# Decoder layer with pooling, dilated attention and 32 experts: router ahead of the second norm, gather tile made on ScalarE, seeds and weight loads moved

## The chip, the cores and the metric

The kernel runs on one core of one Trainium2 chip. The metric is the device time of one execution in microseconds (us). TensorE has an HBM-fed stream of weights beside it, which SyncE issues as DMAs.

## The reference, cut to what matters

One layer, 256 tokens, 1024 channels, everything in f32:

```python
u = layer_norm(x) * (1.0 + scale1) + shift1
...                                            # projection, pooling, attention, gates -> merged
mix = merged @ w_o
x = layer_norm(DN_ALPHA * x + (1.0 + gate1) * mix, ln1_g, ln1_b)
u2 = layer_norm(x) * (1.0 + scale2) + shift2
logits = u2 @ w_router + b_router              # 32 experts, top 4 of them per token, softmax over the 4
# each expert e, for its tokens: h = g * sigmoid(1.702 g) * (up + 1), g = min(u2 @ w_gate + b, 7), ...
ffn = weighted sum over the 4 experts of h @ w_down + b_down
x = layer_norm(DN_ALPHA * x + (1.0 + gate2) * ffn, ln2_g, ln2_b)
```

The three weight matrices of all 32 experts are 4 MB each and are all read: 384 MB.

## The kernel before

The 256 tokens are two tiles of 128 (t = 0, 1). The five engines run hand-written instruction lists side by side and meet at semaphores; `step` on VectorE lets every instruction wait for the one before it.

**Front (0 to 199 us).** Norm, projection, attention and pooling give `gates` (merged, feature-major). Then, in the order of TensorE's list:
- L1449: mix = merged @ w_o, tile by tile, in halves of 512 columns into banks 2 to 5. A logical f32 matmul shows as two passes in the profile.
- L1462: eight transposes of u2 of tile t into banks 6 and 7 (u2 lives in ln_tok, as `xn`). L1470: the rows of gate2, after tile 0. L1477: the router's eight matmuls; L1479: one more that adds the shift and bias row (`shift_sum`) to the logits.
- L1486: the seed of tile t, which puts DN_ALPHA * x into two of banks 0 to 3, onto which the experts' results are added later. L1456: `keep_busy`, dummy matmuls; four (eight passes) after tile 0.
- L1494 to L1497: ranks of the tokens within each expert from the chosen mask and a triangular matrix. L1502: `gather`, which multiplies u2 with a one-hot matrix, so that M_BANK holds the up to 64 tokens of one expert, feature-major. L1558: transposes of the weights per token.
- L1519: `stream`, a unit of the expert's weights (a quarter of 1024 x 1024 is a tile; a unit is four tiles of 512 KB, half a matrix) against those tokens. Six units make one expert: gate 0, 1, up 2, 3, down 4, 5. Between them lie the next expert's gather and the transposes of h (L1540), whose columns are read with a stride of four values.

**VectorE around the change.** For each tile and half: mix times gate1 (L1003), plus DN_ALPHA * x (L1005), statistics (L1008). Then `scaled_norm` (L843: aggregate L845, L846, reciprocal L849, L852, statistics of the result L855), which needs the rows of ln1, and `plain_norm` (L857: aggregate L858, reciprocal L860, and u2 in two halves, L863). Only after both tiles follow the top four of each tile from its logits: max, index, cast, comparison, reduction, cast (L1018 to L1027), then the rank (L1029), `pick_expert` (L1035), and the weights (L1055 to L1060, reduction of 256 values at L1060). ScalarE takes the roots (`norm_std`, L707), copies the transposed tile (L711), makes gate2's rows and the scaled identity (L727, L728), the exponentials of the top four (L717), and turns the gathered tile into the experts' input with scale2 and shift2 (`select_tile`, L737).

**Loads.** SyncE issues the weights in one fixed list and waits for each place to become free. The ring has eight slots of one unit; beside it, units 8 and 9 go to two extra places for the first two turns: `ln_rows` and `x_tok` (extra 0), `late_rows` and `spare_tile` (extra 1). So ten units can be ahead. Slots 4 and 5 (units 4 and 5 of expert 0) become free with the last branch matmul, slots 0 and 1 (units 6, 7) with the mix. In extra 0, `ln_rows` is free when u2 is made and `x_tok` after both seeds (L524, L526). The units 10 and 11 are loaded tile by tile as unit 0 and 1 of expert 0 are used up (L540), every later one when the unit before it in its place is used (L544):

```python
sp.wait_ge(pe_unit_used, AT_PLACE[place - SLOTS] + 1)
sp.dma_start(expert_view(place), source(u)).then_inc(slot_landed[RING[place % SLOTS]], 16)
```

The rows of ln1 are issued by ScalarE once `merged` is complete (L699).

## Time and profile before

| | us |
|---|---|
| median of 3 executions | 1167.73 (1167.57 to 1167.88) |
| the profiled execution | 1166.89 |
| its span, first to last instruction | 1165.0 |
| TensorE busy, passes of weights and matmuls | 1126.5 (97%) |
| VectorE busy | 345.1 (30%) |
| ScalarE busy | 127.3 (11%) |
| DMA over the span | 462.01 MB, mean 397 GB/s |

Times in the profile are counted from the first instruction. An engine's busy time is the union of its instructions; a releaser behind an arrow is the work that ended the wait. PE is TensorE, PEld its weight loads, DVE VectorE, ACT ScalarE, POOL GpSimd, SPq SyncE's list of DMA issues. The granted clock of TensorE has a mean of 0.997 of full speed.

### The profile page before, as it was taken

Reading aid. Unit: us, or ns where it says so; the run is one execution under the profiler, and the core shown is the slowest. Engines: PE = TensorE matmul, PEld = TensorE weight load, DVE = VectorE, ACT = ScalarE, POOL = GpSimd, SP = SyncE. Lnnn points to the kernel's source line nnn. Section 1 sums busy time; section 2 is a strip of 40 time slices with the busy share of each in tenths; the row PEclk is TensorE's granted clock in tenths of the full one; section 3 lists DMA queues with packets and bytes.
Section 4 is the critical chain, followed back from the end, with each engine's and each line's share of the span. In section 5 each row is a group of like instructions: output and inputs, shape, how many; then the busy total and the mean of one; then the engine's idle time right before and its main releaser. Section 6 shows DMA issues by size and latency. Waiting matters only on the chain.

```text
span 1165.0 us, 13496 instructions
## 1 busy us (share of the span) xinstructions
PE 1126.5 (97%) x5821; PEld 553.7 (48%) x5821; DVE 345.1 (30%) x628; ACT 127.3 (11%) x227; POOL 20.1 (2%) x28
## 2 busy tenths in 40 slices
PE   6999999999999999999999999999999999999996
PEld 4868887454444444444444444444444444444442
DVE  4297963642222211211221112221211121112113
ACT  2113221130001000000000000001000100000001
POOL 0000400000000000000000000000000000000000
PEclk9999999999999999999999999999999999999998
DMA  9999685789999999999999999999999999999994
GB/s 346 387 352 353 242 331 230 283 307 394 426 426 427 425 427 425 429 426 429 434 430 430 431 431 432 432 432 432 432 430 431 432 431 432 432 425 427 426 420 196
DMA packets 53732, 462.01 MB, mean 397 GB/s; under 512 B 5294, under 2 KB 7214, under 8 KB 34746
## 3 DMA queue, kind: packets, MB, share of 16 engines
q1 hardware_dynamic: 50032, 457.19, 94.3%
q10 hardware_dynamic: 3658, 4.20, 1.1%
q8 instruction: 34, 0.56, 0.2%
q14 instruction: 8, 0.07, 0.0%
HBM read 460.33 MB, written 1.05 MB: 396 GB/s over the span
## 4 chain that ended last, share of the span: by engine, by line
PE 75%; DMA 21%; DVE 3%; SPq 1%; issue 0%; ACT 0%; DVEq 0%; ACTq 0%
PE bank L1519 43%; DMA ring<-w_up 19%; PE bank L1502 8%; PE bank L1350 6%; PE bank L1546 4%; PE bank L1287 4%; PE bank L1651 2%; PE bank L1435 2%; PE bank L1344 2%; DMA pool_region<-ln_b 1%; DMA ring<-w_in 1%; PE bank L1540 1%; PE bank L1527 1%; SPq L475 1%; PE bank L1508 1%; PE bank L1375 0%
## 5 line engine op out<-in xcount | busy, mean ns | idle before, releaser
L1519 PE MATMUL bank<-ring,feat_region 128*64 128x512 f32 x2848 | 625.2, 595 | 14.3 <-DMA ring<-w_up 14.3
L1519 PEld LDWEIGHTS bank<-ring,feat_region 128*64 128x64 f32 x2848 | 199.5, 137 | 415.7 <-issue 394.9
L1502 PEld LDWEIGHTS bank<-row_region,ln_tok 128*128 128x128 f32 x1024 | 116.8, 192 | 20.3 <-issue 19.7
L1502 PE MATMUL bank<-row_region,ln_tok 128*128 128x64 f32 x1024 | 121.1, 277 | 0.2 <-DVE row_region L1035 0.2
L1100 DVE TENSOR_TENSOR gate_region<-bank,row_region 128x512 f32<-128x512 f32 x31 | 21.4, 691 | 249.4 <-PE bank L1519 249.4
L1078 DVE TENSOR_SCALAR gate_region<-bank 128x512 f32<-128x512 f32 x31 | 21.4, 691 | 200.9 <-PE bank L1527 200.9
L1090 DVE TENSOR_SCALAR acc_region<-bank 128x512 f32<-128x512 f32 x31 | 21.4, 692 | 170.6 <-PE bank L1527 170.6
L1350 PE MATMUL bank<-feat_region,ring 128*128 128x256 f32 x320 | 70.6, 381 | 0.0
L1546 PE MATMUL bank<-gate_region 64*128 64x512 f32 x264 | 65.9, 616 | 0.8 <-DVE gate_region L1123 0.8
L1350 PEld LDWEIGHTS bank<-feat_region,ring 128*128 128x128 f32 x320 | 60.4, 190 | 10.9 <-issue 3.1
L753 ACT ACTIVATE gate_region<-bank 128x256 f32<-128x256 f32 x31 | 11.9, 383 | 470.1 <-PE bank L1508 470.1
L758 ACT ACTIVATE feat_region<-bank 128x512 f32<-128x512 f32 x31 | 18.5, 597 | 331.6 <-PE bank L1540 331.6
L1287 PE MATMUL bank<-feat_region,ring 128*128 128x256 f32 x192 | 42.4, 381 | 1.1 <-DMA ring<-w_in 1.1
L1095 DVE TENSOR_TENSOR feat_region<-bank,small 128x512 f32<-128x512 f32 x31 | 21.4, 691 | 69.0 <-PE bank L1502 69.0
L1287 PEld LDWEIGHTS bank<-feat_region,ring 128*128 128x128 f32 x192 | 36.2, 190 | 6.9 <-DMA ring<-w_in 1.3
L1546 PEld LDWEIGHTS bank<-gate_region 64*128 64x128 f32 x264 | 22.6, 186 | 22.0 <-issue 16.5
L1449 PE MATMUL bank<-ring,gate_region 128*128 128x512 f32 x64 | 27.6, 593 | 0.0
L879 DVE SCALAR_TENSOR_TENSOR row_region<-ring,small,row_region 128x512 f32<-128x512 f32 x32 | 27.1, 848 | 1.1
L1527 PE MATMUL bank<-bias_parts,attn_region 96*64 96x512 bf16 x128 | 25.5, 391 | 0.0
L879 DVE SCALAR_TENSOR_TENSOR acc_region<-ring,small,acc_region 128x512 f32<-128x512 f32 x32 | 24.1, 752 | 1.1
L1088 DVE TENSOR_TENSOR acc_region<-acc_region,gate_region 128x512 f32<-128x512 f32 x31 | 21.3, 686 | 5.8 <-ACT acc_region L756 5.8
L1097 DVE TENSOR_TENSOR feat_region<-feat_region,small 128x512 f32<-128x512 f32 x31 | 21.5, 692 | 1.1
(240 smaller groups left out, 611.9 us busy)
## 6 DMA issues: line engine op xcount, KB each, us to landing
ring<-w_gate SPq DMA_DIRECT2D x16, 4096.0 KB, 27.6
ring<-w_up SPq DMA_DIRECT2D x16, 4096.0 KB, 30.6
ring<-w_down SPq DMA_DIRECT2D x16, 4096.0 KB, 31.7
ring<-w_gate SPq DMA_DIRECT2D x28, 2048.0 KB, 15.5
ring<-w_up SPq DMA_DIRECT2D x26, 2048.0 KB, 15.2
ring<-w_down SPq DMA_DIRECT2D x26, 2048.0 KB, 17.9
ring<-w_ada SPq DMA_DIRECT2D x8, 2048.0 KB, 15.9
ring<-w_in SPq DMA_DIRECT2D x6, 2048.0 KB, 13.9
```

The costliest lines, as they stand in the source:

```text
L879: ins = nc.vector.scalar_tensor_tensor(out=acc, in0=w[:, k, :], scalar=c_silu[:, k:k + 1], in1=acc, op0=ALU.mult, op1=ALU.add)
L1097: nc.vector.tensor_tensor(x_sel, x_sel, shift2.unsqueeze(2).to_broadcast([P, KT, CAP]), ALU.add) \
L1287: last = nc.tensor.matmul(dst[:, q * S:(q + 1) * S], w[:, k, f * P:(f + 1) * P], u_t[:, k, :], start=(q, k) == (0, 0), stop=(q, k) == (1, ...
L1344: last = nc.tensor.matmul(dst[:, cols], u_t[:, k, t * P:(t + 1) * P], w[:, k, :], start=k == 0, stop=k == KT - 1)
L1350: last = nc.tensor.matmul(dst[:, q * S:(q + 1) * S], w[:, k, f * P:(f + 1) * P], u_t[:, k, :], start=k == 0, stop=k == KT - 1)
L1435: last = nc.tensor.matmul(bank[b + n % 2][:, q * S:(q + 1) * S], w[:, k, f * P:(f + 1) * P], src[:, k, :], start=k == 0, stop=k == kk - 1)
L1449: last = nc.tensor.matmul(bank[2 + 2 * t + hf][:, :], gates[:, k, t * P:(t + 1) * P], unit_view(u)[:, k % 4, hf * HALF:(hf + 1) * HALF], s ...
L1502: last = nc.tensor.matmul(M_BANK[:, k * CAP:(k + 1) * CAP], u2[:, t, k * P:(k + 1) * P], pick_tok[:, b, t, :], start=t == 0, stop=t == NT - 1)
L1519: last = nc.tensor.matmul(dst[hf * CAP:(hf + 1) * CAP, :], lhs(k0 + k), cols(tiles[k], hf), start=first and k == 0, stop=last_one and k == 3)
L1527: last = nc.tensor.matmul(dst[hf * CAP:(hf + 1) * CAP, :], pick_bias[:, b, :], half_cols(bias_parts[:, which, :], hf), start=False, stop=stop)
L1546: last = nc.tensor.matmul(bank[2 * t + hf][:, :], scatter_t[rows, b, t, :], values[rows, :], start=False, stop=stop)
L1651: last = nc.tensor.matmul(dst[hf * CAP:(hf + 1) * CAP, :], lhs(4 * (k % 2) + kt), cols(tiles[kt], hf), start=first and kt == 0, stop=last_ ...
```

## The change

1. `scaled_norm` writes its last step in two parts that hold four of the eight feature tiles each (strided columns), signals each (`z_ready`), and only then takes the statistics. TensorE transposes x_tok itself (columns 32 bytes apart), not u2, into `u2_t` in gate_region, and multiplies with the router.
2. The logits are put right afterwards: VectorE adds minus the mean times the column sums of the scaled router, multiplies with the reciprocal root and adds the shift row. Both rows are summed over the partitions by one matmul after the first part of the mix; the matmul of the shift row per tile goes.
3. `second_norm` computes mean and reciprocal root only. ScalarE makes u2, in two activations of 1024 values per tile, after its copies for the router. The root of the second norm of tile 1 comes behind those copies.
4. Mix of tile 1: parts of 512, 256 and 256 columns (banks 4, 5, 0), statistics of tile 1 in quarters.
5. The top four are compared straight with the index (no cast) for both tiles; the picks themselves (bf16) go to the rank matmuls (twelve, not three); the reduction over k is one of 256 values.
6. TensorE's list: the seed of tile 0 waits for all parts of the mix to be read; three dummy matmuls instead of four; the first expert's gather is split into two halves (banks 7 and 6), the second half, the transposes of the weights and the seed of tile 1 lie inside the gate stream of expert 0.
7. Loads: extra 0 is feat_region and ln_rows in place of ln_rows and x_tok. Its first half is issued when the last gate job is done, late_rows ahead of slot 4, the rows of ln1 by SyncE between slots 4 and 5, and extra 0's second half when the moments of the second norm of tile 1 are there. x_sel, h and h_t move to gate_region.

```diff
-        extra_tiles = [[ln_rows[:, 0, :], ln_rows[:, 1, :], x_tok[:, 0, :], x_tok[:, 1, :]],
+        feat_rows = feat_region[:, :].rearrange("p (k n) -> p k n", k=2)
+        extra_tiles = [[feat_rows[:, 0, :], feat_rows[:, 1, :], ln_rows[:, 0, :], ln_rows[:, 1, :]],
...
+        mix_parts = [[(0, HALF, bank[2]), (HALF, D, bank[3])],
+                     [(0, HALF, bank[4]), (HALF, HALF + S, bank[5]), (HALF + S, D, bank[0])]]
...
-            for m in range(SLOTS - 2):
+            for m in range(4):
                 fill_slot(m)
+            sp.wait_ge(job_done, JOB_POOL)
+            sp.dma_start(feat_rows, source(SLOTS)[:, 0:2, :]).then_inc(extra_landed[0], 16)
             sp.wait_ge(job_done, JOB_POOL + 2)
             sp.wait_ge(router_scaled, 1)
             sp.dma_start(late_rows, source(SLOTS + 1)[:, 0:3, :]).then_inc(extra_landed[1], 16)
+            fill_slot(4)
             sp.wait_ge(merged, KT // 2)
+            for r, w in enumerate((ln1_g, ln1_b)):
+                sp.dma_start(ln_rows[:, r, :], w.to_broadcast([P, D])).then_inc(ld_ln1, 16)
+            fill_slot(5)
             sp.dma_start(spare_tile, source(SLOTS + 1)[:, 3, :]).then_inc(extra_landed[1], 16)
             for m in range(SLOTS - 2, SLOTS):
                 fill_slot(m)
-            sp.wait_ge(u2_ready, 2 * NT)
-            sp.dma_start(ln_rows, source(SLOTS)[:, 0:2, :]).then_inc(extra_landed[0], 16)
-            sp.wait_ge(seeded, 2 * NT)
-            sp.dma_start(x_tok[:, :, :], source(SLOTS)[:, 2:4, :]).then_inc(extra_landed[0], 16)
+            sp.wait_ge(moments_ready, 2 + 2 * NT)
+            sp.dma_start(ln_rows, source(SLOTS)[:, 2:4, :]).then_inc(extra_landed[0], 16)
...
+            def u2_tile(t):
+                act.wait_ge(norm2_ready, t + 1)
+                tile = u2[:, t, :].rearrange("p (k a) -> p k a", k=KT)
+                nc.scalar.activation(tile, x_tok[:, t, :].rearrange("p (a k) -> p k a", k=KT), ACT.Identity,
+                                     bias=minus_mean[:, t:t + 1]).then_inc(act_chain, 1)
+                act.wait_ge(act_chain, t + 1)
+                nc.scalar.activation(u2[:, t, :], u2[:, t, :], ACT.Copy, scale=rstd[:, t:t + 1]).then_inc(u2_ready, 1)
...
             for b in range(2):
                 u2_t_half(1, b)
+            norm_std(1, 1)
+            u2_tile(1)
+            nc.scalar.activation(small[:, 102:103], eps, ACT.Exp)
...
+                step(nc.vector.scalar_tensor_tensor(out=row, in0=scale_row, scalar=minus_mean[:, t:t + 1],
+                                                    in1=bank[4 + t][:, 0:NE], op0=ALU.mult, op1=ALU.add), moe_chain)
+                step(nc.vector.scalar_tensor_tensor(out=row, in0=row, scalar=rstd[:, t:t + 1], in1=shift_row,
+                                                    op0=ALU.mult, op1=ALU.add), moe_chain)
...
                     if k % 4 == 0:
-                        pe.wait_ge(u2_ready, 2 * t + k // 4 + 1)
+                        pe.wait_ge(z_ready, 2 * t + k // 4 + 1)
                     last = nc.tensor.transpose(bank[6 + k // 4][:, (k % 4) * P:(k % 4 + 1) * P],
-                                               u2[:, t, k * P:(k + 1) * P], ident)
+                                               x_tok[:, t, :].rearrange("p (a k) -> p k a", k=KT)[:, k, :], ident)
...
                 if t == 0:
-                    keep_busy(4)
+                    pe.wait_ge(scaled_ready, 1)
+                    pe.wait_ge(mix_read, MIX_PARTS)
+                    seed(0)
+                    keep_busy(3)
...
             pe.wait_ge(picked, 1)
-            gather(0).then_inc(gather_done, 1)
-            pe.wait_ge(weight_ready, 1)
+            pe.wait_ge(u2_ready, NT)
+            first_gather(0)
+
+            def weights_and_seed():
+                pe.wait_ge(weight_ready, 1)
...
+                pe.wait_ge(gate2_ready, 1)
+                seed(1)
...
+                               between=(lambda: first_gather(1), weights_and_seed)[k] if first and j == 0
+                               else None) \
```

## Rows read from the trace of the kernel before

**Rows 1.** windows view, two long stretches (window, then busy us of each engine, granted clock, DMA share, GB/s)
```profile
273.00:728.00 455.00, 455.00 (x2382) 194.18 (x2378) 93.99 (x177) 35.73 (x56) 0.00 (x0) 1.00 1.00 428
728.00:1100.00 372.00, 358.94 (x1880) 153.80 (x1878) 75.69 (x143) 25.79 (x43) 0.00 (x0) 1.00 1.00 431
```

**Rows 2.** DMA view of 180 to 300 us, 40 slices of 3 us
```profile
GB/s 426 426 186 0 5 0 87 355 415 414 401 401 352 65 0 55 311 431 437 336 218 309 8 318 314 363 427 352 404 431 262 306 431 426 431 426 437 418 423 442
```

**Rows 3.** windows view, slices of 2 us
```profile
270.00:272.00 2.00, 2.00 (x12) 0.58 (x9) 0.00 (x0) 0.00 (x0) 0.00 (x0) 1.00 0.67 287
272.00:274.00 2.00, 2.00 (x12) 0.72 (x10) 0.00 (x0) 0.00 (x0) 0.00 (x0) 1.00 0.68 139
```

**Rows 4.** timeline of the DMA issues on SyncE (start us, us, line, what)
```profile
248.20 6.34 SPq L540 DMA_DIRECT2D ring<-w_down  x8
258.39 3.76 SPq L544 DMA_DIRECT2D ring<-w_gate  x2
271.79 3.76 SPq L544 DMA_DIRECT2D ring<-w_up  x2
```

**Rows 5.** timeline of TensorE from 226 to 255 us (xcount of passes)
```profile
226.68 1.04 PE L1462 MATMUL bank<-const,ln_tok 128*128 128x128 f32 x8
...
228.65 1.97 PE L1477 MATMUL bank<-router_w,feat_region 128*128 128x32 f32 x16
230.46 0.39 PE L1479 MATMUL bank<-router_w,const 128*128 128x32 f32 x2
231.10 1.99 PE L1486 MATMUL bank<-x_tok,acc_region 128*128 128x512 f32 x4 [0.25 <-ACT acc_region L728]
232.92 3.21 PE L1456 MATMUL bank<-const 128*128 128x454 f32 x8
236.25 1.46 PE L1462 MATMUL bank<-const,ln_tok 128*128 128x128 f32 x8
237.69 1.94 PE L1477 MATMUL bank<-router_w,feat_region 128*128 128x32 f32 x16
...
242.72 3.79 PE L1502 MATMUL bank<-row_region,ln_tok 128*128 128x64 f32 x32 [0.19 <-DVE row_region L1035]
246.43 0.63 PE L1558 MATMUL bank<-const,attn_region 128*32 128x128 f32 x8
247.09 7.09 PE L1519 MATMUL bank<-ring,feat_region 128*64 128x512 f32 x32
...
254.33 0.44 PE L1508 MATMUL bank<-const,row_region 128*128 128x128 f32 x2
```

**Rows 6.** timeline of VectorE, steps around tile 1 and the top four
```profile
218.29 0.21 DVE L845 BATCH_NORM_AGGREGATE small<-small 128x2 f32<-128x12 f32 x1 [2.93 <-DMA pool_region<-ln_b]
...
227.65 0.69 DVE L1003 TENSOR_TENSOR ln_tok<-bank,row_region 128x512 f32<-128x512 f32 x1
...
229.83 0.21 DVE L845 BATCH_NORM_AGGREGATE small<-small 128x2 f32<-128x12 f32 x1
...
239.96 0.20 DVE L1018 MAX8 attn_region<-bank 128x8 f32<-128x32 f32 x1 [1.08 <-PE bank L1479]
...
242.11 0.23 DVE L1029 SCALAR_TENSOR_TENSOR attn_region<-bank,attn_region 128x64 f32<-128x64 f32 x1 [0.30 <-PE bank L1497]
242.37 0.29 DVE L1035 TENSOR_TENSOR row_region<-const,attn_region 128x128 f32<-128x128 f32 x1
...
243.43 0.60 DVE L1060 TENSOR_REDUCE attn_region<-attn_region 128x64 f32<-128x256 f32 x1
```

**Rows 7.** lines 1462 and 1540, weight loads (ns min/median/max), and the first transposes of h
```profile
L1462 PEld LDWEIGHTS bank<-const,ln_tok x16: 138/141/146, 226.2 to 237.3; 128*128 128x128 f32 x16
...
L1540 PEld LDWEIGHTS bank<-const,feat_region x20: 212/216/233, 265.5 to 377.3; 128*128 128x128 f32 x20
...
265.56 0.68 PE L1540 MATMUL bank<-const,feat_region 128*128 128x128 f32 x4
```

**Rows 8.** timeline of ScalarE, a copy of 512 values
```profile
236.94 0.60 ACT L711 ACTIVATE feat_region<-bank 128x512 f32<-128x512 f32 x1 [0.28 <-PE bank L1462]
```

More of the change, by code:

```diff
@@ L1007, in _ @@
                                                         op0=ALU.mult, op1=ALU.add))
-                    step(nc.vector.bn_stats(stats[:, t, hf, :], x_tok[:, t, cols]))
+                    if t == 0:
+                        step(nc.vector.bn_stats(stats[:, t, n, :], x_tok[:, t, cols]))
+                    else:
+                        for q in range(c0 // S, c1 // S):
+                            step(nc.vector.bn_stats(last_stats[:, q, :], x_tok[:, t, q * S:(q + 1) * S]))
                 dve.wait_ge(ld_ln1, 32)
-                scaled_norm(t, 2 + 2 * t + 1)
@@ new lines, in _ @@
+                step(nc.vector.max(top_v[:, t, :], row), moe_chain)
+                step(nc.vector.max_index(top_i[:, t, :], top_v[:, t, :], row), moe_chain)
+            dve.wait_ge(acc_read, 8)
+            for t in range(NT):
+                step(nc.vector.tensor_tensor(picks[:, t], experts,
+                                             top_i[:, t, 0:TOP_K].unsqueeze(2).to_broadcast([P, TOP_K, NE]),
+                                             ALU.is_equal), picks_ready)
+            step(nc.vector.tensor_reduce(chosen_f, picks.rearrange("p t k e -> p t e k"), AX.X, ALU.add), moe_chain)
@@ L1028, in _ @@
+            step(nc.vector.tensor_scalar(top_n.unsqueeze(2), top_v[:, :, 0:1], -1.0, None, ALU.mult), top_ready)
             dve.wait_ge(rank_done, 1)
@@ L1190, in _ @@
                 dve.wait_ge(final_std, t + 1)
-                final(nc.vector.reciprocal(rstd[:, t:t + 1], std[:, t:t + 1]))
+                step(nc.vector.reciprocal(rstd[:, t:t + 1], std[:, t:t + 1]))
                 for hf in range(2):
@@ L1456, in keep_busy, with seed @@
                     nc.tensor.matmul(bank[b][:, 0:columns], ident, const[:, 0:columns], start=True, stop=True)
+            pe.wait_ge(row_sums_ready, 2)
+            def seed(t):
+                for n in (2 * t, 2 * t + 1):
+                    nc.tensor.matmul(bank[n][:, :], scaled_ident, x_tok[:, n // 2, (n % 2) * HALF:(n % 2 + 1) * HALF],
+                                     start=True, stop=False)
             for t in range(NT):
@@ new lines, in _ @@
+            keep_busy(1, 3, S)
+            for t in range(NT):
+                pe.wait_ge(picks_ready, t + 1)
+                if t == 0:
+                    for k in range(TOP_K):
+                        nc.tensor.matmul(Y_BANK[:, 0:NE], tri_bf, picks[:, 0, k, :],
+                                         start=k == 0, stop=k == TOP_K - 1)
+                for k in range(TOP_K):
+                    last = nc.tensor.matmul(Y_BANK[:, NE:2 * NE], tri_bf if t else one_bf[:, 0:1].to_broadcast([P, P]),
+                                            picks[:, t, k, :], start=(t, k) == (0, 0), stop=(t, k) == (1, TOP_K - 1))
@@ L1499, in gather, with gather_tile @@
+            last.then_inc(rank_done, 1)
+            def gather_tile(dst, b, k):
+                for t in range(NT):
+                    last = nc.tensor.matmul(dst, u2[:, t, k * P:(k + 1) * P], pick_tok[:, b, t, :],
+                                            start=t == 0, stop=t == NT - 1)
+                return last
             def gather(b):
                 for k in range(KT):
-                    for t in range(NT):
-                        last = nc.tensor.matmul(M_BANK[:, k * CAP:(k + 1) * CAP], u2[:, t, k * P:(k + 1) * P],
-                                                pick_tok[:, b, t, :], start=t == 0, stop=t == NT - 1)
@@ L1504, in gather, with first_gather @@
-                return last
+                    last = gather_tile(M_BANK[:, k * CAP:(k + 1) * CAP], b, k)
+                return last
+            def first_gather(half):
+                for k in range(4 * half, 4 * half + 4):
+                    last = gather_tile(FIRST_GATHER[half][:, (k % 4) * CAP:(k % 4 + 1) * CAP], 0, k)
+                return last.then_inc(first_gathered, 1)
             def transpose_scatter():
@@ L1513, in out_cols, with stream @@
                 return tile[:, hf * HALF:(hf + 1) * HALF]
-            def stream(dst, lhs, tiles, k0, first, last_one, cols=half_cols, tile_done=None):
+            def stream(dst, lhs, tiles, k0, first, last_one, cols=half_cols, tile_done=None, between=None):
                 for k in range(4):
+                    if k == 2 and between is not None:
+                        between()
                     for hf in range(2):
```

205 lines of the change are left out of this document (92 added, 113 removed).

## The prediction

> **What bounds the kernel now.** I read the long stretches first. From 273 to 728 us TensorE has no gap, and the DMA moves 428 GB/s. From 728 to 1100 us TensorE is busy 358.94 of 372 us, and the DMA moves 431 GB/s [rows 1]. TensorE walks through one expert in about 27.9 us, and the 12.58 MB of an expert's weights take 29.2 us at 431 GB/s. So TensorE, which begins with ten units of two megabytes in place, uses that lead up until 728 us and waits for weights from there. The DMA is the limit in both stretches. The end is therefore the moment at which the DMA stands idle for the last time, plus all that is still to be loaded. A microsecond won on TensorE after that moment is worth nothing.
>
> So the second view is the DMA over 180 to 300 us, in slices of 3 us [rows 2]. It is empty from 189 to 201 us, from 219 to 227 us, and around 247 us. The reader might add these holes up. They don't count by themselves, though: ten units of weights (two megabytes each, six to an expert) are all that fits ahead, and each later unit waits for TensorE to free a place. The last hole is the short one at 270 to 274 us, where the share is 0.67 and 0.68 [rows 3]. What ends it is the issue at 271.79 us [rows 4], which waited for TensorE to finish unit 4 of expert 0 (the first half of its down projection). Both units of the up projection were freed by 261.8 us, their refills (4.9 us each) ran out by 271, and then the queue was empty. From 274 us it is never empty again: TensorE frees 12.58 MB per 27.9 us, the DMA needs 29.2. Remaining bytes agree: the first 14 of 192 units aside, 374 MB at 429 GB/s are 872 us, from 273 to 1145.
>
> **So one number decides:** when TensorE comes to unit 4 of expert 0. From the end of expert 0's gate stream (the transposes of the scatter at 254.33 us [rows 5]) to there, nothing is changed by the edit. I follow TensorE to that point in both kernels.
>
> **What lies around it.** In the kernel before, VectorE waits 2.93 us for the rows of ln1 [rows 6], is 0.5 us late for the last part of the mix (227.65 us, where TensorE is already at the next transposes at 226.68), and then holds TensorE until 236.25 us with both norms. TensorE fills this time with router matmuls of tile 0, the seed of tile 0 and eight dummy passes, which end as the second norm ends: transposes of tile 1 at 236.25 us [rows 5].
>
> **The change, part by part, on TensorE.**
> 1. Mix. One matmul of 64 columns for the row sums (two passes; like the passes of the gather, 3.71 us for 32, 0.12 us each) adds 0.25 us. Sixteen passes of 512 columns become 32 of 256: between nothing and 0.3 us more (a weight load of 190 ns must hide behind a pass of 216), I take 0.15. Transposes of tile 0 start 0.40 us later: 227.08.
> 2. Transposes now read x_tok with 32 bytes between elements; u2 was contiguous. Rows 7 show both kinds: the contiguous weight load takes 141 ns, the one of h, 16 bytes apart, 216 ns. Eight contiguous passes last 1.04 us in all [rows 5], 0.13 each; four of h 0.68 [rows 7], 0.17 each. With only four the end of the last weighs more, so I take 0.035 of the 0.04 (bounds: nothing, and the whole 75 ns). Eight here: +0.28. Transposes and gate2 rows took 1.97 us (226.68 to 228.65), now 2.25: router matmuls of tile 0 start at 229.33.
> 3. They took 1.81 us (228.65 to 230.46): 231.14. The matmuls of the shift row fall away, and the wait for the scaled identity too: it followed the aggregate of tile 1 (229.83, [rows 6]) by 1.27 us. With ln1 early VectorE is free when the mix ends; a last part of 256 columns costs about 0.45 us per step instead of 0.73, so that aggregate comes at 228.75 and the identity at 230.0. Seed of tile 0: 231.10 to 232.92 before, 1.82 us, now until 232.96. Six dummy passes instead of eight, 0.38 each: 2.29, until 235.25. VectorE has the tile for the router (both halves written) at about 232.1: the aggregate, 1.28 us, the reciprocal, and twice 0.78. So the bound changes hands here. **TensorE itself is late by three microseconds**, and of the four that VectorE is earlier (236.2 to 232.1) it sees 1.00 (236.25 to 235.25).
> 4. Tile 1: transposes to first router matmul 1.44 us, plus four strided transposes, 0.14: 236.83. Router matmuls to VectorE's first step 2.27 us (237.69 to 239.96), less two passes: 2.04, so 238.87, where it was 239.96. ScalarE takes the root only behind its two copies (0.60 each [rows 8], to 237.2); then VectorE needs 0.4 and 1.0 us for tile 0, done at about 238.9. Nothing lost, with no room left.
> 5. VectorE, from there to the gather. Before: 2.76 us (239.96 to 242.72). Now: two steps on 32 values (0.23 each), max and index (0.54), two comparisons (0.29 and step costs, 0.66), the reduction, now of 256 values and ahead of the ranks (0.60, [rows 6]), the negation (0.18), rank (0.26), pick to gather (0.35): 3.05. Copy, cast and one reduction are gone. The ranks' twelve small matmuls run beside the reduction. Gather at 241.95, 0.8 us earlier. ScalarE's u2 for tile 1: from 237.8, two activations of 1024 elements; twice the 0.60 us of 512 is the upper bound, so ready by 240.3. Hidden by 1.6 us.
> 6. First half of the gather 1.86 us, then 0.66 us to the first weight tile (246.43 to 247.09): the gate stream starts at 244.47, **2.6 us earlier** than before.
> 7. Inside that stream now lie the other half of the gather (1.86), the weights' transposes (0.66), and the seed of tile 1 (1.82), which before ran at 239.7 to 241.7 us beside VectorE's top four and cost nothing. Its cover is gone. 7.24 + 4.34 us: the stream is through at 256.05 where it was 254.33. **TensorE is 1.7 us later.**
>
> **The DMA's own changes** cost and give nothing. Half of extra unit 0 into feat_region at 176 us and the three late tiles at 179 us fill some six microseconds of the first hole, the same bytes are then missing behind 214 us, and the second hole grows. The rows of ln1, behind fill 4 only, are there by about 209 us, needed at 215.4. The second half of extra unit 0 leaves at about 234 us. Tile releases of unit 0 come earlier (248.20 before), so their refills are through sooner, and the queue stands empty for longer before unit 4. What is late next is this release, at 271.8 + 1.7 = 273.5 us.
>
> **Sum.** The profiled execution took 1166.89 us (span 1165.0), 0.84 below the median of 1167.73. 1166.89 + 1.7 = 1168.6, against the median 1169.4.
>
> A rule weighed against it: the Trainium skill, SBUF — State Buffer, Door 1, says that memory lines have 16 bytes and every access that crosses to a new line pays. By it 32 bytes apart costs what 16 bytes cost, as I took it; by the contiguous price alone the sum would be 0.4 less. VectorE's step that reads x_tok at this stride takes 0.75 us, like those that read it contiguously, so on that engine the trace shows no such cost.
>
> **The rivals.**
> A. Early release counts: expert 0 starts 2.6 us earlier and the holes filled early pay. Then 1167.7 - 2.6 = 1165.1, faster. For it: three large holes [rows 2]. Against: the hole at 270 to 274 lies behind all of them. It needs my TensorE sum to be wrong by over 3 us. Chance 0.15, with all else that ends below.
> B. It cancels: TensorE's passes are shorter at steps 1, 2 and 7 (a pass of 454 columns takes 0.38 us, so four of 512 at 0.43 make a seed of 1.73; contiguous price for transposes, no cost for halves), some 0.9 less: 1168.5 to 1167.8. No change. Chance 0.2.
> C. Slower, by the strided weight loads: if 32 bytes cost twice the surcharge of 16 (150 ns, not 75), and all of it shows, 0.075 us more each than I took: 0.6 more at tile 0, 0.3 at tile 1, since TensorE is the late engine there. 1170.3. It decides from about 0.06 us more each on. For it: 216 against 141 ns; against: no row shows a load at 32 bytes, and as many values are read. Chance 0.15, with small steps mis-sized upwards.
> D. ScalarE's u2 comes late: only if an activation with this stride takes over 2.0 us, 1.6 us of room is used up; at 2.6 us each the gather waits 1.2 more: 1170.6. Chance 0.05.
> E. The clock: it is granted in full in every stretch around [rows 1, 3], and gaps of up to 1.0 us don't lower it. Now TensorE waits for some 1.7 of 3 us before the gather. If it fell to 1.2 GHz over the first half gather and two tiles, they would take 3.6 us more: 1173.0. Chance 0.05. The Trainium skill, TensorE: Matmul & The Clock Gate, Part 1, says that idle time halves the clock and work restores it; by it this risk exists, and no row here shows matmuls at the lower level.
>
> **How the numbers follow.** About 0.2% (2.3 us) is what a measurement of this kernel can tell from no change: 1165.4 and 1170.1. The forecast, TensorE 1.0 to 2.5 us later, has 0.40 and its own range 1168.7 to 1170.2, nearly all within the bound. Faster: A, 0.15. Same: forecast 0.37 and B 0.20. Slower: C, D, E and the forecast's edge, 0.28. The range takes in A's price and leaves out E: 1165.1 to 1171.4.
>
> **What would show it.** Right: TensorE's transposes of tile 1 follow the dummy passes without a wait, while VectorE has written the tile about 3 us earlier; their weight loads near 216 ns; gate stream from about 244.5 us but ending near 256; the DMA's last hole before the issue for unit 4, now near 273.5; from there everything moved by the same amount. Wrong: a gate stream ending before 254, no hole near 272, or a hole later than this one.

## The result and the profile after

The changed kernel takes 1172.81 us (median of 5 executions, 1172.00 to 1173.95), the kernel before 1167.73 us (5 executions beside it on the same chip, 1166.23 to 1168.25). The ratio is 1.0047, with a 95% interval of 1.0036 to 1.0058: **slower, by 5.1 us**, where 1169.4 was forecast. The profiled execution took 1172.81 us, with a span of 1171.0; of before, 1166.89 and 1165.0. The mean granted clock is 0.993, where it was 0.997. The span is 6.0 us longer, and that difference is to be explained. It is more than the 5.1 us of the medians, since the profiled execution of before was 0.84 us under its median and that of the changed kernel was not.

The first view is again the DMA's, the same 40 slices of 3 us as in [rows 2], and SyncE's issues, as in [rows 4]:

```profile
GB/s 426 431 418 438 280 0 55 339 392 389 410 378 4 0 0 0 279 431 431 412 199 0 3 217 165 380 320 317 180 421 431 371 60 311 415 431 437 437 437 410
```

```profile
248.08 12.50 SPq L554 DMA_DIRECT2D ring<-w_down  x8
264.43 3.76 SPq L558 DMA_DIRECT2D ring<-w_gate  x2
277.82 3.76 SPq L558 DMA_DIRECT2D ring<-w_up  x2
```

The reader is to see the last hole: slice 33 (276 to 279 us) with 60 GB/s, where it was slice 31 with 262. Unit 4 of expert 0 is let go at 277.82 us. It was 271.79, so 6.03 us later, and the span grew by 6.0. From the release to the end there are 893.2 us in both kernels (1165.0 - 271.79, 1171.0 - 277.82). So the number that the prediction followed decides, and what is left is why TensorE had finished unit 4 only at 277.82 us and not at 273.5.

TensorE's timeline from the mix to the end of the first gate stream, as in [rows 5]:

```profile
227.33 1.04 PE L1493 MATMUL bank<-const,x_tok 128*128 128x128 f32 x8
...
229.31 1.97 PE L1508 MATMUL bank<-router_w,gate_region 128*128 128x32 f32 x16
231.12 1.96 PE L1486 MATMUL bank<-x_tok,acc_region 128*128 128x512 f32 x4
232.92 2.45 PE L1481 MATMUL bank<-const 128*128 128x454 f32 x6
235.20 1.05 PE L1493 MATMUL bank<-const,x_tok 128*128 128x128 f32 x8
236.59 1.94 PE L1508 MATMUL bank<-router_w,gate_region 128*128 128x32 f32 x16 [0.33 <-ACT gate_region L721]
238.36 0.68 PE L1481 MATMUL bank<-const 128*128 128x256 f32 x2
240.08 0.27 PE L1522 MATMUL bank<-acc_region,attn_region 128*128 128x32 bf16 x4 [1.04 <-DVE acc_region L1053]
...
240.52 1.02 PE L1481 MATMUL bank<-const 128*128 128x256 f32 x2
241.81 3.67 PE L1530 MATMUL bank<-row_region,ln_tok 128*128 128x64 f32 x16 [0.28 <-DVE row_region L1065]
246.07 3.68 PE L1559 MATMUL bank<-ring,gate_region 128*64 128x512 f32 x8 [0.59 <-ACT gate_region L761]
249.68 2.60 PE L1530 MATMUL bank<-row_region,ln_tok 128*128 128x64 f32 x16
252.21 3.65 PE L1559 MATMUL bank<-ring,gate_region 128*64 128x512 f32 x16
255.79 0.63 PE L1601 MATMUL bank<-const,attn_region 128*32 128x128 f32 x8
256.36 1.98 PE L1486 MATMUL bank<-x_tok,acc_region 128*128 128x512 f32 x4
...
260.37 0.44 PE L1546 MATMUL bank<-const,row_region 128*128 128x128 f32 x2
```

Up to the gather every start lies within 0.25 us of the step that forecast it: 227.33 for 227.08, 229.31 for 229.33, 231.12 for 231.14, 232.92 for 232.96, 235.20 for 235.25, 236.59 for 236.83, 241.81 for 241.95. Then the same instruction takes different times: sixteen passes of the gather 3.67 us and then 2.60; eight passes of the stream 3.68 us, sixteen 3.65. The two dummy passes of 256 columns take 0.68 us at 238.36 and 1.02 at 240.52. The windows say why (the granted clock is the third number from the end):

```profile
236.00:238.00 2.00, 1.67 (x16) 1.50 (x14) 0.69 (x4) 1.70 (x4) 0.00 (x0) 1.00 1.05 451
238.00:240.00 2.00, 1.04 (x7) 0.64 (x6) 1.66 (x9) 1.97 (x2) 0.31 (x1) 1.00 0.90 381
240.00:242.00 2.00, 1.65 (x15) 0.87 (x16) 1.59 (x6) 1.98 (x2) 0.00 (x0) 0.68 0.68 287
242.00:244.00 2.00, 2.00 (x11) 2.00 (x11) 1.06 (x4) 0.80 (x6) 0.00 (x0) 0.50 0.03 12
...
248.00:250.00 2.00, 2.00 (x8) 0.39 (x4) 0.00 (x0) 0.00 (x0) 0.00 (x0) 0.50 0.46 96
250.00:252.00 2.00, 2.00 (x15) 2.00 (x15) 0.00 (x0) 0.00 (x0) 0.00 (x0) 0.76 0.82 229
```

**The clock is at its lower level, 1.2 GHz, from about 240.7 to about 251 us.** Ahead of it TensorE is busy 1.04 of 2 us: it waits 1.04 us for the comparisons of tile 1 on VectorE, where the seed of tile 1 stood in the kernel before. This is rival E. Two lines of ScalarE and one of VectorE complete the view:

```profile
237.41 2.15 ACT L734 ACTIVATE ln_tok<-x_tok,small 128x1024 f32<-128x1024 f32 x1 [0.30 <-DVE small L886]
239.58 1.15 ACT L737 ACTIVATE ln_tok<-ln_tok,small 128x1024 f32<-128x1024 f32 x1
```

```profile
216.00 0.21 DVE L869 BATCH_NORM_AGGREGATE small<-small 128x2 f32<-128x12 f32 x1
```

ScalarE's strided activation takes 2.15 us and the contiguous one 1.15. u2 is nevertheless ready at 240.7, 1.1 us ahead of the gather. The wait for ln1 (2.93 us in [rows 6]) is gone, as the change means it to be.

### The profile page after: what moved, and what is told of

Same layout as the page of the kernel before. It is cut to its first block, busy times and chain, and to the rows that moved or that the text cites. A ratio compares the mean times of both kernels' runs of the same rounds, so it can differ in the third digit from the quotient of the medians.

```text
span 1171.0 us, 13544 instructions
## 1 busy us (share of the span) xinstructions
PE 1131.2 (97%) x5844; PEld 558.7 (48%) x5844; DVE 343.6 (29%) x629; ACT 134.0 (11%) x233; POOL 20.7 (2%) x28
## 3 DMA queue, kind: packets, MB, share of 16 engines
HBM read 460.33 MB, written 1.05 MB: 394 GB/s over the span
## 4 chain that ended last, share of the span: by engine, by line
PE 78%; DMA 19%; DVE 2%; ACT 0%; issue 0%; DVEq 0%; ACTq 0%
PE bank L1559 43%; DMA ring<-w_up 19%; PE bank L1530 8%; PE bank L1371 6%; PE bank L1586 4%; PE bank L1308 4%; PE bank L1470 2%; PE bank L1699 2%; PE bank L1456 2%; PE bank L1365 2%; PE bank L1580 1%; PE bank L1567 1%; PE bank L1289 1%; PE bank L1546 1%; DMA small<-c 0%; PE bank L1396 0%
## 5 line engine op out<-in xcount | busy, mean ns | idle before, releaser
L1559 PE MATMUL bank<-ring,gate_region 128*64 128x512 f32 x2848 | 627.4, 596 | 14.8 <-DMA ring<-w_up 14.2
L1559 PEld LDWEIGHTS bank<-ring,gate_region 128*64 128x64 f32 x2848 | 199.2, 137 | 416.9 <-issue 396.2
L1530 PE MATMUL bank<-row_region,ln_tok 128*128 128x64 f32 x1024 | 123.6, 280 | 0.3 <-DVE row_region L1065 0.3
L782 ACT ACTIVATE gate_region<-bank 128x512 f32<-128x512 f32 x31 | 18.5, 597 | 331.5 <-PE bank L1580 331.5
L1125 DVE TENSOR_TENSOR gate_region<-bank,small 128x512 f32<-128x512 f32 x31 | 21.4, 691 | 68.9 <-PE bank L1530 68.9
L1470 PE MATMUL bank<-ring,gate_region 128*128 128x512 f32 (+1 forms) x80 | 27.9, 508 | 0.0
L1122 DVE SCALAR_TENSOR_TENSOR gate_region<-acc_region 128x512 f32<-128x512 f32 x31 | 21.5, 692 | 1.1
```

The lines of the kernel that those rows point to most:

```text
L1122: nc.vector.scalar_tensor_tensor(out=h, in0=up_c, scalar=1.0, in1=sig, op0=ALU.add, op1=ALU.mult).then_inc(h_ready, 1)
L1470: last = nc.tensor.matmul(dst[:, 0:c1 - c0], gates[:, k, t * P:(t + 1) * P], unit_view(u)[:, k % 4, c0:c1], start=k == 0, stop=k == KT - 1)
L1530: last = nc.tensor.matmul(dst, u2[:, t, k * P:(k + 1) * P], pick_tok[:, b, t, :], start=t == 0, stop=t == NT - 1)
L1559: last = nc.tensor.matmul(dst[hf * CAP:(hf + 1) * CAP, :], lhs(k0 + k), cols(tiles[k], hf), start=first and k == 0, stop=last_one and k == 3)
```

## The experiments

Three questions: is it the pause ahead of the ranks that lowers the clock; what do the other parts (seed, halves, dummies, loads) cost or give; and does only the release of unit 4 count. Medians and ratios are against runs of the kernel before on the same chip.

### The pause filled

```diff
-            keep_busy(1, 3, S)
+            keep_busy(2, 3)
             for t in range(NT):
...
-            keep_busy(1, 4, S)
+            keep_busy(1, 4)
             pe.wait_ge(picked, 1)
```

> The changed kernel, with TensorE's wait between the router's last matmuls and the gather filled by more dummy passes (six passes of 454 columns in place of four of 256). Theory (the clock): the granted clock stays at 1.00 from 236 to 256 us, the first half of the gather takes 1.9 us instead of 3.7, the release of unit 4 comes near 273.5 us instead of 277.8, and the profiled span falls from 1171.0 to 1166.7 +- 0.6, 1168.5 in time. Rival (the clock falls for another cause, such as the small router and rank matmuls themselves): it falls to 0.50 again near 241 us and the span stays at 1171 or above.

Measured: span 1166.8 us, clock 0.998, median 1169.16 (1168.21 to 1171.08), ratio 1.0015 (1.0006 to 1.0024). TensorE and SyncE:

```profile
238.04 1.77 PE L1481 MATMUL bank<-const 128*128 128x454 f32 x4
...
241.50 2.00 PE L1530 MATMUL bank<-row_region,ln_tok 128*128 128x64 f32 x16 [0.29 <-DVE row_region L1065]
...
256.03 0.44 PE L1546 MATMUL bank<-const,row_region 128*128 128x128 f32 x2
```

```profile
273.49 0.33 SPq L558 DMA_DIRECT2D ring<-w_up  x1
```

Only dummy work was added, and 4.2 us of the span went (by the two ratios to the kernel before, 3.7). The half gather takes 2.00 us for 3.67, the gate stream ends at 256.03 where the prediction had 256.05, and unit 4 is let go at 273.49 where it had 273.5. Two small errors cancel in that match: the gather begins 0.45 us before the 241.95 of the prediction, and from the start of the stream to its end are 11.95 us, not 11.58. The miss of the changed kernel is the clock all the same: 277.82 - 273.49 = 4.33 us, of which 0.31 is an earlier front (all that lies ahead of the gather) in this execution (gather at 241.50) and 4.0 the lower level. Five of the ten executions lie at 1168.2 to 1168.7 us with a mean clock of 0.998, three at 1169.6 to 1169.8 with 0.997, and two near 1171 with 0.996, so the filling does not seem to hold the clock every time.

### The seed of tile 1 back in its old place

```diff
-            keep_busy(1, 3, S)
+            pe.wait_ge(gate2_ready, 1)
+            seed(1)
             for t in range(NT):
...
-                pe.wait_ge(gate2_ready, 1)
-                seed(1)
```

> The changed kernel, with the seed of tile 1 moved out of expert 0's gate stream to where it was before, between the router's last matmuls and the ranks. Theory (clock plus 1.8 us of uncovered work): the clock is held by real work in the gap, the gate stream of expert 0 ends near 254.1 us, unit 4 is released near 271.6, span 1164.8 +- 0.6, the kernel ends level with the one before. Rival (the clock needs more than this): 0.50 again, and the span only falls by the 1.8 us of the seed, to 1169.2. Rival (the seed's place is free because its passes were hidden): as with the dummies alone, 1166.7.

Measured: span 1164.7, release at 271.62 us; 1.87 us before the filled variant's. From the gather to the release are 30.08 us here and 31.99 in the filled variant, so the seed inside the stream costs 1.91 us. The median is 1168.96, ratio 1.0006 (0.9997 to 1.0015), and hides two groups: five executions at 1166.6 to 1167.2 us, all with a mean clock of 0.997, and five at 1169.0 to 1169.9 us with 0.995 or 0.996 (an eleventh at 1170.3, with 0.997). The profiled one is of the first group, so the trace doesn't show where the others lose the clock. The seed covers the pause ahead of the ranks; TensorE then still waits 0.62 us ahead of the gather and 0.59 behind its first half.

### The six dummy passes behind the first seed left out

```diff
                     seed(0)
-                    keep_busy(3)
```

This is the variant above without these three matmuls.

> As the one with the seed of tile 1 moved back, and without the six dummy passes behind the seed of tile 0, for which TensorE kept VectorE waiting. Theory (TensorE was the late engine there, by 2.9 us): transposes of tile 1 start near 232.9 us in place of 235.2, the gather near 239.6, unit 4 is released 2.2 us earlier than in that kernel, span 1162.6 +- 0.8, faster than the kernel before by 2.3 us. Rival (those passes held the clock): the clock falls to 0.50 somewhere between 233 and 245 us and takes back 3 to 4 us: span 1166 or more.

Measured: median 1165.40 (1164.34 to 1166.06), ratio 0.9978 (0.9969 to 0.9987), span 1163.8 with the front 0.64 us later in the profiled execution (transposes of tile 0 at 227.68), mean clock 0.997 or 0.998 in all eleven.

```profile
233.27 1.04 PE L1493 MATMUL bank<-const,x_tok 128*128 128x128 f32 x8
```

The transposes of tile 1 still have no wait, 2.3 us earlier against those of tile 0. The span is above the 1162.6 +- 0.8 that was expected: the late front is 0.64 us of that, and from the release (269.96) to the end are 893.8 us, 0.6 more than in the kernel before. What those 0.6 us are is not settled. **The dummies ran while VectorE's tile was ready**: it was written at 232.3 us in the changed kernel and TensorE took it up at 235.20. That the clock never falls here is measured; why it holds without these passes and falls in half of the executions with them is not settled.

### The loads issued in the old order

```diff
-            sp.wait_ge(job_done, JOB_POOL)
-            sp.dma_start(feat_rows, source(SLOTS)[:, 0:2, :]).then_inc(extra_landed[0], 16)
...
             fill_slot(5)
+            sp.wait_ge(router_scaled, 1)
+            sp.wait_ge(job_done, JOB_POOL + 2)
+            sp.dma_start(late_rows, source(SLOTS + 1)[:, 0:3, :]).then_inc(extra_landed[1], 16)
...
             sp.wait_ge(moments_ready, 2 + 2 * NT)
+            sp.dma_start(feat_rows, source(SLOTS)[:, 0:2, :]).then_inc(extra_landed[0], 16)
```

On top of the variant with the seed back (the rows of ln1 stay early).

> As the one with the seed of tile 1 moved back, but the early half of extra unit 0 and the three late tiles are issued where the kernel before had them (behind the moments of tile 1, and behind slot 5). Theory (only the release of unit 4 counts): the DMA's hole at 189 to 201 us is whole again, the one at 214 to 227 us shrinks, and the span is that of the kernel with the seed moved back, within 0.5 us. Rival (bytes moved into an early hole are won): 2.5 to 6 us slower than that kernel.

Measured: span 1164.9, release 271.67 (271.62 with the early loads), the same two groups (1166.4 to 1167.2 and 1169.0 to 1169.7 us), median 1168.09, ratio 1.0007 (0.9997 to 1.0016) against 1.0006 with the early loads. Filling the first hole early is worth nothing that these runs can tell.

### The kernel before with only the seed of tile 1 moved

```diff
                 if t == 0:
+                    seed(0)
                     keep_busy(4)
...
             last.then_inc(weight_t_done, 1)
+            pe.wait_ge(gate2_ready, 1)
+            seed(1)
```

> The kernel before, with one edit of the change alone: the seed of tile 1 is taken from between the router's last matmuls and the ranks and put behind the weights' transposes, ahead of expert 0. Theory (the uncovered seed and the wait it leaves, which lowers the clock): the granted clock falls to 0.50 near 241 us for about 10 us, unit 4 is released 1.8 + 4 us later, near 277.5, span 1170.8. Rival (the seed counts, the clock falls only with the changed kernel's smaller matmuls and longer wait): clock 1.00, span 1166.8.

Measured: median 1174.23 (1173.36 to 1174.46), ratio 1.0060 (1.0045 to 1.0075), span 1172.2, release 279.06, mean clock 0.991.

```profile
241.86 0.18 PE L1495 MATMUL bank<-attn_region 128*128 128x32 bf16 x1 [1.91 <-DVE attn_region L1026]
...
242.94 6.97 PE L1503 MATMUL bank<-row_region,ln_tok 128*128 128x64 f32 x32
249.84 1.07 PE L1559 MATMUL bank<-const,attn_region 128*32 128x128 f32 x8
250.84 3.59 PE L1484 MATMUL bank<-x_tok,acc_region 128*128 128x512 f32 x4
```

```profile
240.00:242.00 2.00, 0.14 (x4) 0.17 (x4) 1.64 (x8) 0.06 (x1) 0.00 (x0) 0.61 0.79 320
242.00:244.00 2.00, 2.00 (x11) 1.60 (x8) 1.65 (x6) 0.33 (x2) 0.00 (x0) 0.50 0.02 8
```

The old kernel's gather, 3.79 us in [rows 5], takes 6.97, its transposes 1.07 for 0.63, the seed 3.59 for 1.99. One move, with nothing else of the change, lowers the clock and costs more than the whole change does. It costs 1.4 us more than was expected, since the whole gather, the transposes and the seed all ran at the lower level: 3.2, 0.3 and 1.7 us more than at the full clock.

### Dummies early, later, and later still

Three dummy matmuls (six passes, 2.3 us) ahead of the next gather, in the kernel before: in expert 0, in expert 2, and in expert 8.

```diff
                     pe.wait_ge(picked, i * BODY + (j + 2))
+                    if first and j == 0:
+                        keep_busy(3, 7)
                     gather(1 - b)
```

(`j == 2` for expert 2; `at == 2 and j == 0` for expert 8.)

> The kernel before, with three dummy matmuls (six passes of 454 columns, 2.3 us) ahead of the gather inside expert 0, before its unit 4. Theory (the end is the release of unit 4 plus a constant): release near 274.1 us, span 1165.0 + 2.3 = 1167.3. Rival (TensorE's lead of several experts hides it): span 1165.0.

> The kernel before, with the same three dummy matmuls (2.3 us) in the same place of expert 2. Theory (behind the DMA's last hole TensorE's time is free): release of unit 4 of expert 0 unchanged at 271.8 us, span 1165.0 +- 0.4. Rival (every microsecond of TensorE up to 728 us counts): 1167.3.

> The kernel before with the same three dummy multiplications (2.3 us) in expert 8, behind both narrow places (release of unit 4 near 272 us, and the transfers near 440 us that the dummies in expert 2 opened). Theory: the transfers have a lead of several us there and are never idle, so the span is the release of unit 4 plus 893.2 us within 0.4 (1165 us if the front part runs as in the profiled execution of before). Rival (TensorE's own time after the front counts): 1167.3 or more by the same sum.

Measured: in expert 0 median 1169.37, ratio 1.0019 (1.0009 to 1.0028), release 274.99; in expert 2 median 1168.85, ratio 1.0012 (1.0002 to 1.0021), release 272.70; in expert 8 median 1167.52, ratio 0.9997 (0.9987 to 1.0006), release 271.80 and span 1164.9 = 271.80 + 893.1. In the profiled executions of the first two the front was 0.9 us late (the first issue behind it at 249.11, before 248.20), so expert 0's dummies moved the release by 274.99 - 272.70 = 2.29 us, what they last. Spans: 1168.2 and 1166.9. So early dummies cost their full time and the latest nothing, as the theory has it, but **those in expert 2 cost some of it**, which it did not foresee: 1166.9 - 272.70 = 894.2, not 893.2, so 1.0 of 2.3 us in the profiled execution (1.6 us by the medians). The windows of that kernel at 441 us:

```profile
441.00:442.00 1.00, 1.00 (x6) 0.29 (x4) 0.00 (x0) 0.00 (x0) 0.00 (x0) 1.00 0.43 180
442.00:443.00 1.00, 1.00 (x8) 0.40 (x6) 0.00 (x0) 0.00 (x0) 0.00 (x0) 1.00 0.27 115
```

```profile
442.24 3.76 SPq L544 DMA_DIRECT2D ring<-w_gate  x2
```

The two extra places are used for the first turns alone. Where they fall away, one issue comes 21 us behind the one before it; in the last kernel of the three, at 439.06, it still comes in time. That is a second narrow place, with a lead of about one microsecond (1.3 by this run: 2.3 us were lost and 1.0 showed). The release near 272 us ends the last hole only as long as TensorE loses little between the two.

### Needed work in place of the filler

The variant without the six dummy passes, and half of the first seed behind the ranks in place of the dummy there, and VectorE's negation moved behind the first pick.

```diff
-                    seed(0)
+                    seed(0, 0)
...
-            keep_busy(1, 4, S)
+            seed(0, 1)
             pe.wait_ge(picked, 1)
...
-            step(nc.vector.tensor_scalar(top_n.unsqueeze(2), top_v[:, :, 0:1], -1.0, None, ALU.mult), top_ready)
...
             pick_expert(0, 0).then_inc(picked, 1)
+            step(nc.vector.tensor_scalar(top_n.unsqueeze(2), top_v[:, :, 0:1], -1.0, None, ALU.mult), top_ready)
```

> As the one without the dummy passes (seed of tile 1 in its old place), with the second half of the seed of tile 0 behind the ranks in place of the dummy there, and the negation for the exponentials behind the first pick. Theory: transposes of tile 1 start when VectorE has the tile, 0.5 us earlier, the gather another 0.2 us, unit 4 is released 0.7 us earlier than in that kernel (measured from the first transposes of tile 0), span 1163.0 or below, 0.3 to 0.4% faster than the kernel before. Rival (the clock has no more room without the passes ahead of the transposes): it falls to 0.50 and the span is 1166 or more.

Measured: median 1164.73 (1163.53 to 1165.16), ratio 0.9979 (0.9970 to 0.9988), span 1161.7, clock 0.997 in all eleven executions.

```profile
238.13 2.00 PE L1530 MATMUL bank<-row_region,ln_tok 128*128 128x64 f32 x16
240.72 1.94 PE L1559 MATMUL bank<-ring,gate_region 128*64 128x512 f32 x8 [0.59 <-ACT gate_region L761]
```

```profile
268.21 3.76 SPq L558 DMA_DIRECT2D ring<-w_up  x2
```

Both seeds are now ahead of the gather, no filler is left there, and the gather begins 4.6 us before the old one's 242.72. From the first transposes of tile 0 (226.72 here, 227.68 in the variant without the dummies) to the release are 0.8 us less, as expected. The medians don't show it: the ratio is 0.9979, and 0.9978 for that variant on another chip, and the 0.3 to 0.4% that were expected are 0.2.

### The gather undivided

```diff
             first_gather(0)
+            first_gather(1)
...
-                               between=(lambda: first_gather(1), weights_and_seed)[k] if first and j == 0
+                               between=(None, weights_and_seed)[k] if first and j == 0
```

> d1_best with the first gather undivided again (all eight passes ahead of the stream, the weights and the last seed still behind unit 0). Theory (only the release of unit 4 counts): the eight passes are the same ones, so the first tile of unit 0 is let go about 2 us later, unit 4 at the same time within 0.5 us of d1_best's 268.21, and the span is 1161.7 within 0.5. Rival (the halves are worth something): the ring's transfers behind the first tile wait 2 us longer, and the span is 1163.5 or more.

Measured: median 1163.94 (1162.75 to 1163.97, 5 executions), ratio 0.9962 (0.9949 to 0.9975), span 1161.0, a little below the 1161.7 +- 0.5 that was expected: the lowest ratio of the study, 0.38% below before, though the intervals of the last two variants overlap.

```profile
238.43 3.79 PE L1530 MATMUL bank<-row_region,ln_tok 128*128 128x64 f32 x32
242.14 5.37 PE L1559 MATMUL bank<-ring,gate_region 128*64 128x512 f32 x24
247.44 0.63 PE L1602 MATMUL bank<-const,attn_region 128*32 128x128 f32 x8
```

```profile
243.26 7.05 SPq L554 DMA_DIRECT2D ring<-w_down  x8
...
267.56 3.76 SPq L558 DMA_DIRECT2D ring<-w_up  x2
```

From the gather to the weights' transposes are 9.01 us here (238.43 to 247.44), 9.97 in halves (238.13 to 248.10). In halves TensorE waits 0.59 us for ScalarE's copy of the first half, which otherwise lies beside the second half's passes, and two short groups of passes are slower than one long. The first tile is let go 1.4 us later (243.26 for 241.83) and this costs nothing; unit 4 is let go 0.65 us earlier. So **the halves are a small loss**: 30.08 us from the gather to the release in halves, 29.13 in one.

### Room for two tiles more

Tile 3 of units 14 and 15 goes into the token buffer x_tok once both seeds and u2 have read it; on the order with the gather in halves. The ring's own transfers of these two units then bring three tiles.

```diff
             sp.dma_start(ln_rows, source(SLOTS)[:, 2:4, :]).then_inc(extra_landed[0], 16)
+            sp.wait_ge(sig_c_ready, 2)
+            sp.wait_ge(u2_ready, NT)
+            for n, u in enumerate(ROOM):
+                sp.dma_start(x_tok[:, n, :], source(u)[:, 3, :]).then_inc((ld_c, ld_pos)[n], 16)
```

> d1_best with room for two tiles more: tile 3 of units 14 and 15 goes into the two halves of the token buffer once the seeds and the second norm have read it, ahead of the ring's own transfers, so that unit 4 of expert 0 being let go is waited for two tiles (2.4 us of transfer) later. Simple theory: the hole near 269 us shrinks by 2.4 us, span 1159.3. Refined theory, from the dummies in expert 2: the place near 440 us has a lead of only about 1 us, so the hole moves there, and the gain is about 1 us: span 1160.7. Rival: the four-tile transfers cut in 3 + 1 cost as much as they give, span 1161.7 or more.

Measured: median 1164.10 (1163.61 to 1165.50), ratio 0.9964 (0.9951 to 0.9978), by the medians the same as the undivided gather beside it. The profiled execution was the slowest of the five (span 1163.7, release 268.75). Its windows:

```profile
240.00:242.00 2.00, 1.41 (x11) 0.93 (x11) 1.76 (x7) 1.29 (x5) 0.00 (x0) 1.00 0.98 395
266.00:270.00 4.00, 4.00 (x22) 1.41 (x20) 0.00 (x0) 0.00 (x0) 0.00 (x0) 1.00 0.36 107
278.00:282.00 4.00, 4.00 (x22) 1.36 (x20) 2.35 (x6) 0.99 (x2) 0.00 (x0) 1.00 0.83 322
436.00:437.00 1.00, 1.00 (x6) 0.29 (x4) 0.00 (x0) 0.00 (x0) 0.00 (x0) 1.00 0.54 213
```

and those of the kernel without the room:

```profile
240.00:242.00 2.00, 1.41 (x8) 0.57 (x8) 1.90 (x6) 1.29 (x4) 0.00 (x0) 1.00 0.43 176
266.00:270.00 4.00, 4.00 (x22) 1.29 (x19) 0.00 (x0) 0.00 (x0) 0.00 (x0) 1.00 0.31 70
```

The two tiles do fill the hole behind 240 us (share 0.98 for 0.43). But the one at 266 to 270 is hardly shorter, and that the release that ends it came 0.54 us later in this execution is only a part of the 2.4 us that were to go. New idle time shows at 278 to 282 and at 436 us, the second narrow place. Both kernels moved the same: 363 and 360 GB/s over 226 to 300 us, 423 and 426 over 300 to 450. The five spans are 1161.8 to 1163.7 us. The simple theory's 1159.3 is not reached, and nor is the refined one's 1160.7, though idle time does appear where it expected it. The rival (the transfers of three tiles cost as much as the room gives, 1161.7 or more) is not excluded: no gain from the room is shown. The ratios 0.9964 and 0.9979 come from different chips and their intervals overlap.

## Why the prediction was wrong

**What held.** The DMA bounds the kernel, holes ahead of the last one don't count, and the end is the release of unit 4 plus 893.2 us. That constant was read from one kernel and lies between 893.1 and 893.8 in ten of the twelve others. The exceptions, the dummies in expert 2 (894.2) and the room (895.0), are those in which idle time opened behind that release. Rival A (the early release pays) is out: the loads' order gave 0.05 us, and letting the first tile go 1.4 us later cost nothing.

**Steps 1 to 5** came within 0.25 us each. A part of that is luck: in the variants with the same list ahead of them the transposes of tile 0 start anywhere from 226.72 to 227.68 us, from one execution to the next. Two terms were mis-sized, without effect on the sum, and two sums were slightly off (step 5's terms end at 241.92, not 241.95; the 178 units that remain of 192 are 373 MB, 870 us at 429 GB/s, not 872). In step 2 the weight loads at 32 bytes take 188 ns and the contiguous ones 141 [rows 7], but eight transposes last 1.04 and 1.05 us, as long as the contiguous eight [rows 5]. The surcharge was to be 0.28 and is nothing, so the dearer load doesn't show here; rival C is out. The transposes began 0.25 us later than the 227.08 of step 1, which made up for it. In step 5 ScalarE's pass over x_tok was bounded by twice the 0.60 us of 512 contiguous values; it takes 2.15. That is over the 2.0 from which rival D was to decide, but the second pass takes only 1.15 and u2 is ready at 240.7, so D's room of 1.6 us shrank to 1.1 and stayed.

**Steps 6 and 7 failed, because both took every pass at the full clock.** The terms: the first half of the gather 3.67 us for 1.86, so that the stream starts at 246.07 for 244.47 (+1.6); from there to its end 14.30 us for 11.58 (+2.7). Together 4.3, and 256.05 becomes 260.37. For what the clock adds the sum had no term. From there to the release are 17.45 us, in before 17.46: unit 4 comes at 277.82, not at 273.5. With the pause filled, the clock stays at 1.00 and the two times come out (256.03, 273.49).

**The reasoning that misled** is in rival E: "gaps of up to 1.0 us don't lower it", from rows in which heavy passes stood on both sides. The seed that the change moves away was priced as work (1.8 us inside the stream) and not as what kept TensorE busy between the router and the ranks. In its place stand 0.68 us of dummies of 256 columns, 1.04 us of waiting, and small passes of 32 columns. E's mechanism was right and its chance of 0.05 was too low. Its price came close (3.6 us for the 4.0 that the runs show); that its time of 1173.0 lies 0.2 from the measured median is partly luck, since it starts from the median of before, 0.84 above the execution that was profiled. The rule cited there, from the Trainium skill, TensorE: Matmul & The Clock Gate, Part 1, that idle time halves the clock and work restores it, agrees with the windows shown: 0.50 at and behind the pause, 1.00 again after some ten microseconds of passes.

The whole difference, by terms that the runs measured, against the release of before at 271.79:

| term | us | from |
|---|---|---|
| the gather starts earlier | -0.91 | 242.72, 241.81 |
| gather in halves | +0.96 | 9.97 against 9.01 |
| seed of tile 1 behind the gather | +1.91 | 31.99 against 30.08 |
| lower clock | +4.02 | 277.82 - 273.49 - 0.31 |
| sum | +5.98 | measured +6.03 |

And what the change could give was held back by its six dummy passes: VectorE's three microseconds were there, and without the passes TensorE takes 2.3 of them.

## What to carry to other kernels

Before moving work out of TensorE's list, ask what it covered: a seed or any heavy pass between two waits may be what keeps the clock, and its price elsewhere is its duration plus all passes behind it at the lower level (here 1.9 and 4.0 us). Where such a pause must be, put needed work into it first (the fastest order here has no filler between the seeds), and look at how the executions spread: two groups with two mean clocks say that something lowers the clock in some executions only, and one profiled execution can show either. When DMA bounds a kernel, find its last idle moment and the release that ends it, add the constant behind it, and then check how much lead the next narrow place has before counting on more.

## What the runs showed of the hardware

- **The clock fell at pauses that look harmless.** In the changed kernel it fell near 240.7 us, 0.6 us behind a wait of 1.04 us (TensorE busy 1.04 of 2 us there). In the old kernel with its seed moved it fell near 240.4 us, when 0.5 us of a wait of 1.91 had passed. The lower level then stayed for 10 and for 13.6 us (to 251.0 and 254.1), although TensorE was busy for most of that time. What decides is not settled: the variant with the seed back waited 0.62 us ahead of the gather, with TensorE busy 1.38 of the 2 us from 240, and kept the clock in its profiled execution.
- **At the lower level not all groups double.** Sixteen passes of the gather take 3.67 us for 2.00, eight of the stream 3.68 for 1.94, the seed 3.59 for 1.98. These durations include the modelled end of the last pass; by starts, the undivided gather takes 6.90 for 3.71, eight passes of the stream 3.61 for 1.87.
- **Single values 32 bytes apart were dearer on three engines.** ScalarE takes 2.15 us for 1024 of them and 1.15 for 1024 contiguous ones (the two activations also differ in their function). TensorE's load takes 188 ns for 141, which showed nowhere in the time of the transposes. VectorE has the row that the prediction missed. Its u2 step (L863) reads x_tok 32 bytes apart in 0.75 us for 512 values. The contiguous steps that take as long, such as L852 with 0.75, are of another kind and read two tensors. A step of its own kind, contiguous (L840, from the first norm), takes 0.81 us for twice as many values:

```profile
8.01 0.81 DVE L840 TENSOR_SCALAR ln_tok<-x_tok,small 128x1024 f32<-128x1024 f32 x1
...
235.45 1.54 DVE L863 TENSOR_SCALAR ln_tok<-x_tok,small 128x512 f32<-128x512 f32 x2
```

So "on that engine the trace shows no such cost" was a wrong reading: the values 32 bytes apart took nearly twice as long each. No run changed the stride alone, so that it is the stride is argued, not shown. In the changed kernel VectorE's last step over x_tok takes four neighbouring values out of every eight, and its 0.75 us for 512 are those of the contiguous L852. The Trainium skill, SBUF — State Buffer, Door 1, has every access that crosses to another 16-byte line pay, and four f32 values fill such a line; these rows agree with it, since single values are dearer and groups of four aren't. The size of the cost is not the same everywhere: TensorE's load at 32 bytes (188 ns) is faster than that at 16 bytes in [rows 7] (216 ns), though both cross a line with each value, and why is open.
